# Summing expert rows on TensorE: from one 128x128 diagonal to four 64x64 parts of the array

## The reference, cut to what matters

```
def peer_ffn(h, w_pq, sub_keys, peer_u, peer_v):      # 16384 experts, chunks of 128 tokens
    ...
        q = (hc @ w_pq).reshape(PEER_CHUNK, PEER_HEADS, 2, PEER_DK_HALF)
        sc = jnp.einsum('thcd,chnd->thcn', q, sub_keys)
        vals, idx = lax.top_k(sc, PEER_TOPK)
        ...
        g = jax.nn.softmax(top_s, axis=-1)
        ue = peer_u[experts]
        ve = peer_v[experts]
        act = jax.nn.gelu(jnp.einsum('td,thkd->thk', hc, ue), approximate=False)
        return jnp.einsum('thk,thkd->td', (g * act), ve)
```

## Time and profile before

| | |
|---|---|
| median of the runs | 2927.46 us |
| span of the profiled execution | 2927.4 us |
| PE busy | 2491.4 us (85%) |
| PE weight loads busy | 1743.2 us (60%) |
| DVE busy | 1760.7 us (60%) |
| ACT busy | 1133.8 us (39%) |
| POOL busy | 676.9 us (23%) |
| mean granted PE clock | 0.921 of full |
| read from HBM | 828 MB |
| gathers (line 2160) | 512, first adds on PE at 570 us, last at 2309 us |

### The profile page before, as it was taken

How to read it: one execution, slowest core, us unless ns; L and a number is a source line. 1 busy time by engine, 2 the same in 40 slices (tenths; PEclk the granted TensorE clock), 3 DMA queues, 4 the chain that set the end, 5 groups by cost and what they waited for, 6 DMA issues and landing times.

```text
span 2927.4 us, 29566 instructions
## 1 busy us (share of the span) xinstructions
PE 2491.4 (85%) x10118; PEld 1743.2 (60%) x10118; DVE 1760.7 (60%) x4222; ACT 1133.8 (39%) x2762; POOL 676.9 (23%) x566
## 2 busy tenths in 40 slices
PE   8999999879989759888968678588985799988998
PEld 7786666667755437546736544264763376655883
DVE  2101311598797778666989888878998416412430
ACT  2101301242533765354442578464554325512210
POOL 0000000122234343332223445444223101100000
PEclk9999999989989889999989578799997999999999
DMA  5545243689999999999899989999999743432443
GB/s 197 173 154 168 95 144 129 219 335 351 390 394 417 409 397 392 419 389 384 299 332 402 365 301 385 396 420 419 417 418 416 277 159 109 151 130 88 153 155 116
DMA packets 160966, 838.64 MB, mean 286 GB/s; under 512 B 17400, under 2 KB 21896, under 8 KB 95024
## 3 DMA queue, kind: packets, MB, share of 16 engines
q0 software_dynamic: 73728, 536.90, 45.8%
q1 hardware_dynamic: 82464, 287.75, 28.0%
q10 hardware_dynamic: 4624, 12.11, 1.1%
HBM read 828.27 MB, written 8.41 MB: 286 GB/s over the span
## 4 chain that ended last, share of the span: by engine, by line
PE 55%; DVE 18%; ACT 12%; DMA 11%; issue 4%; POOL 0%; ACTq 0%; DVEq 0%; SPq 0%
PE ps L908 26%; DMA BIG<-in_uv,BIG 10%; PE ps L928 5%; PE ps L929 5%; PE ps L1152 5%; DVE BIG L1943 5%; DVE X L1923 4%; PE ps L909 4%; PE ps L1176 2%; PE ps L1177 2%; ACT L1441 2%; DVE BIG L1854 1%; PE ps L1122 1%; DVE BIG L1851 1%; PE ps L1101 1%
## 5 line engine op out<-in xcount | busy, mean ns | idle before, releaser
L2160 POOL DMA_INDIRECT BIG<-in_uv,BIG x512 | 634.2, 1239 | 1646.3 <-DVE BIG L1900 564.6
L908 PE MATMUL ps<-BIG,RING 128*128 128x256 f32 x3472 | 807.6, 385 | 13.8 <-DMA RING<-in_w_cq 4.9
L908 PEld LDWEIGHTS ps<-BIG,RING 128*128 128x128 f32 x3472 | 670.1, 194 | 133.4 <-issue 28.6
L1943 DVE CUSTOM_DVE_ANT_0 BIG<-BIG 128x1024 f32<-128x1024 f32 x512 | 619.6, 1217 | 85.4 <-DMA BIG<-in_uv,BIG 84.2
L1923 DVE SCALAR_TENSOR_TENSOR X<-BIG,small,X 128x1024 f32<-128x1024 f32 x333 | 426.6, 1281 | 91.7 <-ACT small L1445 91.6
L1441 ACT ACTIVATE small<-small 128x1 f32<-128x1 f32 x512 | 102.6, 200 | 620.7 <-DVE small L1943 619.4
L908 PE MATMUL ps<-WK,RING 128*128 128x256 f32 x1232 | 287.2, 385 | 25.2 <-DVE BIG L1702 23.2
L908 PEld LDWEIGHTS ps<-WK,RING 128*128 128x128 f32 x1232 | 235.7, 193 | 65.3 <-DVE BIG L1702 31.1
L928 PE MATMUL ps<-RING,BIG 128*128 128x512 f32 (+1 forms) x448 | 223.0, 579 | 5.0 <-DVE BIG L1681 2.4
L929 PE MATMUL ps<-RING,BIG 128*128 128x512 f32 (+1 forms) x448 | 222.6, 578 | 0.0
L1274 ACT ACTIVATE BIG<-ps 128x256 f32<-128x256 f32 (+2 forms) x143 | 56.8, 398 | 408.5 <-PE ps L909 343.2
(11 more groups left out here) (259 smaller groups left out, 3136.7 us busy)
## 6 DMA issues: line engine op xcount, KB each, us to landing
RING<-in_w_up SPq DMA_DIRECT2D x88, 512.0 KB, 6.0
RING<-in_w_down SPq DMA_DIRECT2D x66, 512.0 KB, 3.6
RING<-in_w_pq SPq DMA_DIRECT2D x32, 512.0 KB, 6.1
RING<-in_w_cc SPq DMA_DIRECT2D x16, 512.0 KB, 8.1
RING<-in_w_cx SPq DMA_DIRECT2D x16, 512.0 KB, 4.1
RING<-in_w_cb SPq DMA_DIRECT2D x16, 512.0 KB, 4.4
RING<-in_w_cv SPq DMA_DIRECT2D x16, 512.0 KB, 5.0
RING<-in_w_gc SPq DMA_DIRECT2D x16, 512.0 KB, 4.7
```

What stands on the lines that cost most here:

```text
L908: e.matmul(ps[:, 0:256], W[:, j, :], src[:, j, 0:256], start=j == 0, stop=False)
L1943: e.tensor_tensor_reduce(out=u, in0=HF[:, t % 2, :], in1=u, scale=1.0, scalar=0.0, op0=ALU.mult, op1=ALU.add, accum_out=dots[:, k % 8:k % ...
L2160: e.indirect_dma_start(out=slot[i], out_offset=None, in_=I["uv"], in_offset=bass.IndirectOffsetOnAxis(ap=IDX[:, t, c:c + 1], axis=0)).then ...
```

## The change

The same 179 choices are added by PE, at the same places in the order, with smaller matmuls. The diagonal matrix of a choice is stored as 128 partitions x 64 columns: the weights of tokens 0 to 63 on the diagonal of the upper 64x64 block, those of tokens 64 to 127 on the diagonal of the lower one. For this ACT scales a new constant, ident2, of the two 64x64 identities; in the space of four buffers of 128 columns there are now eight of 64. An add is four matmuls, each with 64 partitions of contraction, 64 columns of weights and 512 moving columns: token half by column half. Each uses another quarter of the array: token half 0 reads the partitions 0 to 63 and writes bank 6, token half 1 reads 64 to 127 and writes bank 7; the first 512 columns of half 0 go to the output partitions 0 to 63, the second 512 to 64 to 127, and the other way round for half 1. The total of a group is four DVE instructions of 64x512 in the place of two of 128x512, and POOL prepares ident2 with three instructions at the program's start.

```
-        DIAG = [DG[:, 0, :], DG[:, 1, :], at_(W0 + 15872, 128), at_(W0 + 16000, 128)]
+        DIAG = [DG[:, i // 2, 64 * (i % 2):64 * (i % 2) + 64] for i in range(4)] + [at_(W0 + 15872 + 64 * i, 64) for i in range(4)]
...
@@ tensor_program, add(k)
-                v, d = slot[slot_of[k]][:, 1024:2048], DIAG[pe_turn[k] % 4]
+                v, d = slot[slot_of[k]], DIAG[pe_turn[k] % 8]
                 first, last = k == pe_sums[t][0], k == pe_sums[t][-1]
-                e.matmul(banks[6][:, :], d, v[:, 0:512], start=first, stop=last)
-                e.matmul(banks[7][:, :], d, v[:, 512:1024], start=first, stop=last).then_inc(pacc.sem, pacc("sum", k))
+                for side in range(2):
+                    for half_of in range(2):
+                        rows, to = slice(64 * half_of, 64 * half_of + 64), 64 * (half_of ^ side)
+                        mm = e.matmul(banks[6 + half_of][to:to + 64, :], d[rows, :],
+                                      v[rows, 1024 + 512 * side:1536 + 512 * side], start=first, stop=last)
+                mm.then_inc(pacc.sem, pacc("sum", k))
...
@@ scalar_program, expert(t, c)
-                w.wait_ge(*at["ident"])
-                if n >= 4:
-                    w.wait_ge(*at["sum", pe_order[n - 4]])
-                e.activation(DIAG[n % 4], ident[:, :], ACT.Copy, scale=a).then_inc(gate.sem, gate("gate", k))
+                w.wait_ge(*at["ident2"])
+                if n >= 8:
+                    w.wait_ge(*at["sum", pe_order[n - 8]])
+                e.activation(DIAG[n % 8], ident2[:, :], ACT.Copy, scale=a).then_inc(gate.sem, gate("gate", k))
...
@@ vector_program, total(t)
-                    for hh in range(2):
-                        d = X[:, t, hh * 512:(hh + 1) * 512]
-                        e.tensor_tensor(d, banks[6 + hh][:, :], d, ALU.add).then_inc(dve.sem, dve("total", t))
-                        at["ev", "experts", 6 + hh] = (dve.sem, dve.n)
+                    for half_of in range(2):
+                        rows = slice(64 * half_of, 64 * half_of + 64)
+                        for side in range(2):
+                            to = 64 * (half_of ^ side)
+                            d = X[rows, t, 512 * side:512 * side + 512]
+                            e.tensor_tensor(d, banks[6 + half_of][to:to + 64, :], d, ALU.add).then_inc(dve.sem, dve("total", t))
+                        at["ev", "experts", 6 + half_of] = (dve.sem, dve.n)
...
@@ gpsimd_program
+            e.memset(ident2[:, :], 0.0).then_inc(pool.sem, pool("ident20"))
+            w.wait_ge(*at["ident20"])
+            e.affine_select(out=ident2[:, :], in_=ident2[:, :], compare_op=ALU.not_equal, fill=1.0, base=0, pattern=[[-1, 64]],
+                            channel_multiplier=1).then_inc(pool.sem, pool("ident21"))
...
```

More of the change, by code:

```diff
@@ L503, in program @@
         DG = sb("DG", [128, 2, 128])
+        ident2 = sb("ident2", [128, 64])
         banks = [ctx.enter_context(nc.psum_tensor(f"ps{i}", [128, 512], F32)) for i in range(8)]
@@ L2173, in gpsimd_program @@
                             channel_multiplier=1).then_inc(pool.sem, pool("ident"))
+            e.memset(ident2[:, :], 0.0).then_inc(pool.sem, pool("ident20"))
+            w.wait_ge(*at["ident20"])
+            e.affine_select(out=ident2[:, :], in_=ident2[:, :], compare_op=ALU.not_equal, fill=1.0, base=0, pattern=[[-1, 64]],
+                            channel_multiplier=1).then_inc(pool.sem, pool("ident21"))
+            w.wait_ge(*at["ident21"])
+            e.affine_select(out=ident2[:, :], in_=ident2[:, :], compare_op=ALU.not_equal, fill=1.0, base=-64, pattern=[[-1, 64]],
+                            channel_multiplier=1).then_inc(pool.sem, pool("ident2"))
             w.wait_ge(*at["flip0"])
```

## The result

The changed kernel takes 2905.47 us (median of 4 runs, 2902.87 to 2908.53) against 2926.97 us of the kernel before in the same comparison (4 runs): 21.5 us less, a ratio of 0.9933 with a 95% interval of 0.992 to 0.9946. The forecast was 2897 us, 30 less. The profiled execution took 2902.87 us with a span of 2901.1.

The account below looks back on a forecast made before the run. PE held 55% of the chain, with transfers, gathers and DVE also late from 570 to 2310 us. Adds -34, totals +3, diagonals -2.5, clock +3 make -30 from 2927.4: 2897 us, range 2876 to 2916 (8 in 10: 2872 to 2955).

Parts of the forecast that it names:

- The column halves overlap: Both column halves of the same array rows run at once in an add, so eight records take two slots; chance 0.45.
- the rival: Column halves run one after the other: each add 1.92 us on PE, kernel slower at 2943 us; chance 0.21.
- The rival of half an overlap: Column halves overlap only in one pass each, three slots: add 1.49 us, kernel 2918 us; chance 0.13.
- that of program order: Records of all four parts start as written: add 2.35 us, kernel 2970 us; with worse cases, chance 0.14.
- The add at 1.06 us: In a stream, two slots of 0.86 us together plus 0.20 for array changes, against 1.72: saving 0.66 us, 38%.
- From the add to the whole: 38% of the adds' 117 us of chain is 45 us; less 5.7 and 5.6, 34 us saved.
- its own cuts: No saving at 840-898 or for a quarter of 38 us elsewhere (5.7 us); half at 1450-1600 and 2230-2310 (5.6).
- The cut to a half for 2230 to 2310 us: Between gathers there, adds are 13.7 us of the chain; only half of their 38% saving was counted.
- What is late next: From 705 to 840 us transfers have room: 11 us come through, adds' chain share falls 21.3% to about 14%.
- The totals: Eight more DVE instructions of 0.68 us, 5.4 us; 3 us counted, two groups on a chain; bounds 0 and 5.4.
- The diagonal: ACT's diagonal takes about 350 ns for 402, half of 106 gates on the chain: 2.5 us gain, bounds 0 and 11.
- The clock: With less PE work between waits, more time at the lower clock level: 3 us lost, bounds 0 and 15.

Follow-up runs that it names:

- the same shift: The changed kernel with 268 choices summed on PE for 179: 2907.81 us, ratio 0.9931; group 2 408.6 us for 422.7, group 1 471.6 for 462.2.

## Why the prediction was right, point by point

1. *The column halves overlap: right.* Eight records in 1.09 us; in turn they take 1.93 and the kernel 2944 us, where the rival had 2943. The rival of half an overlap falls by the same rows, and that of program order by both written orders.

2. *The add at 1.06 us: mis-sized.* It costs 1.216. The two slots of 0.43 are as said; the changes between the full array and its parts cost 0.36 us and not 0.20. The prediction fell short of its own rows: 0.09 us before the eight records and 1.08 - 0.86 = 0.22 within and behind them make 0.31. By the timeline after: 0.09 on entry (761.65 instead of 761.56), 0.48 instead of 0.43 between the two slots, 0.02 for the four starts one behind the other, 0.09 on leaving, and 0.10 between the first and the second record of the projection that follows (0.70 - 0.38 = 0.32 instead of 0.22). I had counted only the first and the fourth. The two before a second record were in the earlier trace rows: line 951's four records there last 0.71 us, so, less a record of 0.38, the second pair starts 0.33 after the first and not 0.22, and line 1176 behind them has a first record of 0.70 us where the earlier trace rows have 0.59. It looks as if the first weight load is what stands exposed. In a stream a weight load runs beside the matmul ahead. After a change the trace has the first load start with its own matmul and the second load 0.055 us (64 columns) or 0.107 us (128) behind it, and the first record is longer by 0.05 and 0.10, the same amounts. No run tests this. The saving is 0.50 us or 29%, for 38.

3. *From the add to the whole: right in kind, too high for the late groups.* With 29% the working of the prediction gives 34 of the 117 us, and with its own cuts (34 of 45) 26 us. The profiles show 21.3 + 1.3 with the longer totals in them; with 1.57 us for each of the three totals that begin groups 1 to 3 that is 23 + 4, so 27. In groups 0 and 1 the chain of before was a fair guide: the adds are 9.0% of it in each, 41 + 43 us, 29% of that is 24, and 23 came. The other 33 us of the 117 lay in groups 2 and 3, 29% is 10, and 4 came at most: there the chain ran over an add with a gather or DVE close beside it. The cut to a half for 2230 to 2310 us was too mild: the dot products that start at 2230.3 and 2307.3 us before are 77.5 us apart after, for 77.0.

4. *What is late next: right on the time, wrong on the share.* From 705 to 840 us I had let the whole 11 us through, and with 29% for 38 these are 8.4; the same projections stand 8.0 us closer together. But I had looked only at the transfers' room. The adds' share of the chain fell to 3.8% and not to 14%, since DVE, busy 106 of 135 us, was a bound close behind and has 33.7% there now. A share of the chain says who ends last and not how long the work takes. The gathers' part did not grow by what the adds lost (15.8% for 16.6%), which would have shown me wrong.

5. *The totals: +3 forecast, 4 to 10 measured.* Two sizes were off. Each total costs 1.57 us more and not 1.36, and I had counted two on a chain where the chain after runs through three (groups 0, 1 and 3).

6. *The diagonal: -2.5 forecast.* The instruction takes 348 ns as said. Its worth is not separated from nothing: 2.7 us by the medians, 0.3 by the ratios. One row of the kernel after for it and one for the total:

```profile
L1458 ACT ACTIVATE DG<-ident,small x91: 347/348/350, 565.5 to 2284.7; 128x64 f32<-128x64 f32 x91
```

```profile
L1941 DVE TENSOR_TENSOR X<-ps,X x16: 678/688/695, 1014.6 to 2289.3; 64x512 f32<-64x512 f32 x16
```

7. *The clock: +3 forecast.* It fell from 0.921 to 0.892 on the mean. Groups 2 and 3 show no sign of having paid for it; for groups 0 and 1 it was not tried, so the term stays open. PE waits longer for the gates (line 1180, us and times; then who waited for it), as it arrives earlier:

```profile
  ACT DG L1458: 209.6, 76
  ACT BIG L1458: 129.0, 52
...
  POOL BIG L2168: 444.0, 123
```

338.6 us for the 240.9 of the earlier trace rows. That is where much of the saved PE time lies: 98 us more of waiting. POOL waits 444.0 us for the adds for the 500.6 of the earlier trace rows.

The sum can be held against measurements in two parts. The totals are +7 (4 to 10) for the +3 of the forecast. The adds, the diagonals and the clock together are what the change has over the kernel that differs from before by its totals alone: the ratios 1.0024 and 0.9933 give 27 us, an estimate with some 5 us either way, since the two were not run side by side. The forecast for these three is -34 - 2.5 + 3 = -33.5, and with the add at 1.216 us -25. So the mechanism held, and what was missing from the 30 us lies in two mis-sized terms, the change between full array and parts (8 us) and the totals (4 us); together they are somewhat more than the 8.5 us, within what the measurements leave open. That the forecast was no further off owes something to the cut of a quarter and a half, which were set by judgement. The range that the prediction gives for this case, 2876 to 2916, is not what its own bounds add up to: they give 2927.4 - 45 - 11 = 2871 and 2927.4 - 20 + 5.4 + 15 = 2928.

## What to carry to other kernels

A matmul with a diagonal or otherwise block-wise zero weight matrix can be cut into the quarters of the array that hold its blocks, and the quarters run at once, at the price of some 0.36 us for leaving and re-entering the full array. It pays where the streams are long: 512 columns in float32 gain 0.86 us before that price. With 128 columns, by an estimate from the same figures, the four slots of 0.11 us would become two and gain 0.21, less than the price. Before counting on such a saving, take its share of the chain by stretches and ask of each what else is nearly as busy: here a microsecond of adds was worth 0.4 where PE was busy 84 to 87% of the time, and 0.06 where DVE or the gathers led. When an engine has been relieved, the split of work between engines is worth setting anew, but stretch by stretch: the same shift gained 14 us in one group and lost 9 in another.

## What the runs showed of the hardware that I had not expected

- All four quarters of the array start within 0.02 us of each other although both column halves read the same 64 partitions, and in float32: four records of 512 columns in a slot of 0.43 to 0.48 us.
- The order in which matmuls are written did not bind quarters to one another: with either of two orders an add costs 1.216 us and its first four records start within 0.02 us.
- A change between full array and parts costs 0.36 us in all: 0.09 on entry, 0.09 on leaving, 0.05 and 0.10 between the first and the second record after each change, and 0.02 for the four starts.
- Two DVE instructions of 512 columns from PSUM, 0.68 us long each, start 0.60 to 0.62 us apart when they work on the same partitions, and 0.70 to 0.73 us apart when the partitions change. An instruction over 64 partitions is as long as one over 128.
- The granted clock fell from 0.78 to 0.69 in a stretch in which PE had to do less between the same waits, and to 0.63 with still less, without the stretch getting longer.
